# A diffusion trunk on one core: the gather of the experts placed right after the routing, the test for crowded groups placed ahead of the last scatter, and the last two experts' inner values transposed earlier

## The reference

```python
def _moe(h, router_w, router_b, w_gate, w_up, w_down):
    scores = jax.nn.sigmoid((t @ router_w).astype(jnp.float32))
    sel = scores + router_b.astype(jnp.float32)
    group_score = lax.top_k(sel.reshape(-1, N_GROUPS, EXPERTS_PER_GROUP), GROUP_SCORE_TOPK)[0].sum(-1)
    best_group = jnp.argmax(group_score, axis=-1)
    ...
    hid = jax.nn.silu(jnp.einsum("td,edf->tef", t, w_gate)) * jnp.einsum("td,edf->tef", t, w_up)
    out = jnp.einsum("tef,efd->td", hid * combine[..., None], w_down)
```

## Time and profile before

| | |
|---|---|
| median of three runs | 2187.74 us (2181.6 to 2188.81) |
| the profiled execution, its own time | 2186.74 us |
| its span in the trace | 2184.9 us |
| mean granted clock of TensorE | 0.973 |
| PE busy | 2021.1 us, 92% |
| DVE busy | 1338.0 us, 61% |
| ACT busy | 1034.3 us, 47% |

### The profile page before, as it was taken

How to read it: one execution, slowest core, us unless ns; L and a number is a source line. 1 busy time by engine, 2 the same in 40 slices (tenths; PEclk the granted TensorE clock), 3 DMA queues, 4 the chain that set the end, 5 groups by cost and what they waited for, 6 DMA issues and landing times.

```text
span 2184.9 us, 44966 instructions
## 1 busy us (share of the span) xinstructions
PE 2021.1 (92%) x18880; PEld 1403.4 (64%) x18881; DVE 1338.0 (61%) x2625; ACT 1034.3 (47%) x1783; POOL 246.5 (11%) x363
## 2 busy tenths in 40 slices
PE   6999999898998999899899998998999999988996
PEld 3666666557775675677666665776466666647774
DVE  2656665437896342689822325898656666537896
ACT  3334344226774341676523315766444444326774
POOL 1422222110001000100010001000322232110000
PEclk8999999998999999899999998999999999999998
DMA  9244344345886444488644353888311121125880
GB/s 392 90 152 153 123 146 156 141 156 187 282 322 216 159 172 158 162 309 300 240 150 146 138 190 123 310 303 283 121 46 63 47 70 46 45 80 186 282 303 29
DMA packets 56912, 381.22 MB, mean 174 GB/s; under 512 B 6400, under 2 KB 10624, under 8 KB 12144
## 3 DMA queue, kind: packets, MB, share of 16 engines
q1 hardware_dynamic: 51696, 373.00, 47.7%
q10 hardware_dynamic: 4608, 4.20, 0.6%
q0 software_dynamic: 384, 0.89, 0.1%
HBM read 373.96 MB, written 4.10 MB: 173 GB/s over the span
## 4 chain that ended last, share of the span: by engine, by line
PE 76%; DVE 13%; ACT 5%; issue 4%; DMA 2%; ACTq 0%; SPq 0%; DVEq 0%
PE ps L838 15%; PE ps L1505 6%; DVE e_wlo L2817 5%; PE ps L1509 5%; PE ps L1508 5%; PE ps L788 4%; PE ps L764 4%; PE ps L744 3%; PE ps L979 3%; PE ps L1292 3%; DVE bufx L2835 2%; PE ps L799 2%; PE ps L1461 2%; ACT e_whi L1685 2%; PE ps L1393 2%
## 5 line engine op out<-in xcount | busy, mean ns | idle before, releaser
L2817 DVE TENSOR_TENSOR e_wlo<-ring,e_whi 128x1024 fp32r<-128x1024 f32 x384 | 456.2, 1222 | 90.9 <-ACT e_whi L1685 75.2
L1685 ACT ACTIVATE e_whi<-ring 128x1024 fp32r<-128x1024 f32 x384 | 402.9, 1060 | 117.9 <-PE ps L1509 114.4
L838 PE MATMUL ps<-bufh,ring 128*128 128x384 f32 x1024 | 392.4, 505 | 2.0 <-ACT scratch L1685 0.7
L838 PEld LDWEIGHTS ps<-bufh,ring 128*128 128x128 f32 x1024 | 177.0, 191 | 93.9 <-issue 18.3
L1505 PE MATMUL ps<-e_whi,e_hs 128*128 128x512 f32 x512 | 210.5, 411 | 28.2 <-DVE e_wlo L2817 24.8
L1685 ACT ACTIVATE scratch<-ps 128x384 f32<-128x384 f32 (+6 forms) x311 | 109.0, 368 | 213.2 <-PE ps L838 53.3
L1509 PE MATMUL ps<-e_whi,e_hs 128*128 128x512 f32 x512 | 200.4, 391 | 0.0
L1508 PE MATMUL ps<-e_wlo,e_hs 128*128 128x512 f32 x512 | 200.0, 391 | 0.0
L2946 POOL TENSOR_SCALAR bufx<-bufo,x_gb 128x384 f32<-128x384 f32 x56 | 37.6, 685 | 1072.5 <-DVE bufo L2256 1072.5
L1505 PEld LDWEIGHTS ps<-e_whi,e_hs 128*128 128x128 f32 x512 | 96.0, 188 | 69.1 <-ACT e_whi L1685 43.1
L2349 DVE SCALAR_TENSOR_TENSOR scratch<-scratch,par 128x386 f32<-128x386 f32 x192 | 128.5, 669 | 4.8
(11 more groups left out here) (312 smaller groups left out, 3490.7 us busy)
## 6 DMA issues: line engine op xcount, KB each, us to landing
ring<-in_moe SPq DMA_DIRECT2D x192, 1024.0 KB, 4.9
ring<-in_w_ada SPq DMA_DIRECT2D x96, 1024.0 KB, 6.8
ring<-in_gdn_w_in SPq DMA_DIRECT2D x32, 1024.0 KB, 7.0
ring<-in_gdn_w_out SPq DMA_DIRECT2D x8, 1024.0 KB, 5.0
ring<-in_gqa_w_in SPq DMA_DIRECT2D x6, 1024.0 KB, 5.1
ring<-in_gqa_w_out SPq DMA_DIRECT2D x4, 1024.0 KB, 6.9
ring<-in_mla_w_out SPq DMA_DIRECT2D x4, 1024.0 KB, 7.7
ring<-in_mla_w_in SPq DMA_DIRECT2D x3, 1024.0 KB, 4.9
```

The costliest lines, as they stand in the source:

```text
L838: last = mm(ps[:, head_bank(n, m), 0:T], w[:, m % 2, kt, :], bufh[:, kt, :], start=(kt == 0), stop=(kt == KT - 1))
L1685: return op(out, in_, ACT.Copy, **kw)
L2817: return tt_(e_wlo[:, b, :], w, e_whi[:, b, :].bitcast(F32), ALU.subtract)
```

## The change

It has three parts, all in the mixture of experts.

1. The eight gather pieces of pair 0 leave the table and stand in the code of PE right behind the token tiles: four ahead of the counts and the row of slot numbers, four behind. ACT takes the first four, splits piece 0, copies the row ("r"), takes the other four, and goes on with piece 1.
2. The branch moves. On PE (`crowded_blocks`) and DVE it stands just ahead of the first scatter step of the last group, on ACT behind the last step of the table. The flags are computed later on DVE (`crowded_flags`), after the second pair's `e_pick`, and the two `put_back` go there too. The extra blocks use other buffers (`x_yhi`, `x_ylo`).
3. In the last stretch the transposes of experts 2 and 3 of group 3 move ahead: T(3, 2) behind U(3, 3), and T(3, 3) behind D(3, 1). Each T of an expert other than the group's first also waits for the low part of the transpose before it (`tlo`).

```diff
-MOE_STEPS = [("G", 0, m) for m in range(8)]
+MOE_STEPS = []
...
+    if _x == NE - 1:
+        MOE_STEPS.append(("T", NG - 1, EPG - 2))
     if _late:
         MOE_STEPS.append(("S", _group, 2 * _turn))
     if _x >= 2:
         MOE_STEPS.append(("D", (_x - 2) // EPG, (_x - 2) % EPG))
...
+    if _x == NE - 1:
+        MOE_STEPS.append(("T", NG - 1, EPG - 1))
     if _late:
         MOE_STEPS.append(("S", _group, 2 * _turn + 1))
-    if _x >= 1:
+    if 1 <= _x < NE - 1:
         MOE_STEPS.append(("T", (_x - 1) // EPG, (_x - 1) % EPG))
-MOE_STEPS += [("D", 3, 2), ("T", 3, 3), ("D", 3, 3)] + [("S", 3, q) for q in range(4)]
+MOE_STEPS += [("D", 3, 2), ("D", 3, 3)] + [("S", 3, q) for q in range(4)]
...
-MOE_FOLLOW, MOE_PIECE_OF = [], {}
+MOE_FOLLOW, MOE_PIECE_OF = [("g", 0, m, None) for m in range(4)], {}
...
+            if _p == 1:
+                MOE_FOLLOW.append(("r", 0, 0, None))
+                MOE_FOLLOW += [("g", 0, _m, None) for _m in range(4, 8)]
...
                 token_tile(5)
+                for m in range(4):
+                    gather_piece(l, 0, m)
 
                 pe.wait_ge(sid_ready, l + 1)
...
                 last.then_inc(row2_mm, 1)
+                for m in range(4, 8):
+                    gather_piece(l, 0, m)
...
                     elif kind == "T":
+                        if e:
+                            pe.wait_ge(F["tlo"], n)
                         transpose_hidden(F, n, e % 2)
...
                         if e == 0:
+                            if j == NG - 1:
+                                crowded_blocks(l, comb)
...
                         if j == 0:
                             pick_pair(1)
+                            dve.wait_ge(row2_ready, l + 1)
+                            dve.wait_ge(ax_ready, 2 * l + 2)
+                            put_back(0)
+                            put_back(1)
+                            crowded_flags(l)
...
                     elif kind == "s":
+                        if e == 0 and j == NG - 1:
+                            crowded_blocks(l)
```

More of the change, by code:

```diff
@@ L507, in trunk @@
         x_put = e_hs[:, 2, 1, 0:TT, :].rearrange("p a b -> p (a b)")
+        x_yhi, x_ylo = (e_hs[:, 1, half, :, :].rearrange("p k c -> p (k c)") for half in range(2))
         e_whi, e_wlo = sb("e_whi", [P, SPLITS, PIECE], F32R), sb("e_wlo", [P, SPLITS, PIECE], F32R)
@@ L1533, in scatter_piece @@
                     b = banks[ft % len(banks)]
-                    mm(ps[:, b, 0:T], e_yhi[:, P * ft:P * ft + P], put, start=True, stop=False)
-                    mm(ps[:, b, 0:T], e_ylo[:, P * ft:P * ft + P], put,
+                    hi, lo = (e_yhi, e_ylo) if S is F else (x_yhi, x_ylo)
+                    mm(ps[:, b, 0:T], hi[:, P * ft:P * ft + P], put, start=True, stop=False)
+                    mm(ps[:, b, 0:T], lo[:, P * ft:P * ft + P], put,
                        start=False, stop=True).then_inc(S["sc"], 1)
@@ L1597, in moe @@
                 last.then_inc(row2_mm, 1)
+                for m in range(4, 8):
+                    gather_piece(l, 0, m)
                 comb = e_rt[7].rearrange("p (t e) -> p t e", t=TT)
[L1599 to L1622, removed]
-                                pe.nop()
-                            with pe.Else():
-                                pe.sem_inc(X["ga"], 5)
-                                pe.sem_inc(X["tr"], EPG)
-                                pe.sem_inc(X["wfree"], EPG * PIECES)
-                                pe.sem_inc(X["sc"], KT)
@@ L2102, in y_high @@
                 for y in range(2):
-                    copy(e_yhi[:, 512 * y:512 * y + 512], ps[:, 3 + y, :]).then_inc(S["yhi"], 1)
+                    copy((e_yhi if S is F else x_yhi)[:, 512 * y:512 * y + 512], ps[:, 3 + y, :]).then_inc(S["yhi"], 1)
             def moe(l):
@@ L2735, in route @@
                 pick_pair(0)
-                dve.wait_ge(rk_mm, 2 * l + 2)
-                v.step(V.tensor_copy(e_cnt[:, :], ps[:, 2, 80:84]))
-                v.wait()
-                for b in range(2):
-                    ts_(flags[:, :, b], e_cnt[:, :], float(P * (b + 1)), None, ALU.is_gt)
-                v.step(V.tensor_reduce(m3[:, 46:47], e_cnt[:, :], AX.X, ALU.max))
-                v.wait()
-                ts_(flags[:, 0, 2:3], m3[:, 46:47], float(P), None, ALU.is_gt).then_inc(flags_ready, 1)
                 for n in range(2, 2 * TT):
@@ L2770, in route, with crowded_flags @@
                 dve.wait_ge(comb_ready, l + 1)
-                dve.wait_ge(row2_ready, l + 1)
+            def crowded_flags(l):
+                m3 = e_rt[9]
+                dve.wait_ge(rk_mm, 2 * l + 2)
+                v.step(V.tensor_copy(e_cnt[:, :], ps[:, 2, 80:84]))
+                v.wait()
+                for b in range(2):
+                    ts_(flags[:, :, b], e_cnt[:, :], float(P * (b + 1)), None, ALU.is_gt)
+                v.step(V.tensor_reduce(m3[:, 46:47], e_cnt[:, :], AX.X, ALU.max))
+                v.wait()
+                ts_(flags[:, 0, 2:3], m3[:, 46:47], float(P), None, ALU.is_gt).then_inc(flags_ready, 1)
             def pick_pair(pair):
```

94 lines of the change are left out of this document (64 added, 30 removed).

## The result

The changed kernel takes 2168.95 us, the median of 6 runs (2166.31 to 2177.65), and the kernel before, on the same chip, 2182.91 us (6 runs, 2180.86 to 2188.81). The ratio is 0.9925 with an interval of 0.9903 to 0.9947: by it the change saves 16.4 us, and anything from 11.6 to 21.2 fits the interval; the two medians differ by 14.0. The profiled execution took 2167.08 us with a span of 2165.3, where before it was 2186.7 and 2184.9. The direction is as predicted, and the time lies just inside the forecast's lower bound of 2168; the gain is twice the forecast 8.2 us.

A forecast was written before the change was run, and what follows sets the result against it. PE was taken to set the pace inside the mixture, with time to be had only at its two ends. 22.2 - 3.4 - 5.8 + 10 - 12.8 - 2 = 8.2 us gained, forecast 2180 us, range 2168 to 2190.

The forecast's parts named there:

- the head: Last token copy to first expert matmul: gathering at once takes 10.1 us a layer, gaining 22.2 us for four.
- the transposes: Last stretch: earlier transposes end PE's waits, about 1.0 us remains ahead of D(3, 3); gain 10 us for four.
- the clock at the tail: Behind D(3, 3): idle time brings half clock in the scatter; loss 2 us for four.
- Piece 1 and the moved work: Inside the mixture: later piece 1 loses 3.4 us, DVE's work moved to step "w" loses 5.8 us, for four.
- The branch at the tail: Ahead of the last scatter: DVE's branch makes the first addition 3.2 us later; loss 12.8 us for four.
- rival 4: Branch fetch at the tail waits behind weights: 2.05 us longer erases the gain, 4 us longer gives 2196; chance 0.10.
- rival 2: DVE's moved work is covered and the gather runs at full clock in all four layers; 2170 us; chance 0.10.
- Rival 1: At the tail the flag is loaded and the branch target fetched while D(3, 3) runs; 2167 us; chance 0.08.
- rival 3: Gather stays at half clock until the low half, or scatter and sums run at half clock; 2183 to 2187; chance 0.20.

The follow-up runs named there:

- e5: Changed kernel with the flags and two `e_put` on DVE moved from step "w" to between the splits of pieces 0 and 1; 2173.62 us, ratio 0.9922.
- e6: Changed kernel with ACT splitting piece 1 ahead of the row's copy and the four low gathered pieces; 2166.18 us, ratio 0.9921.
- e8: Changed kernel with DVE's moved work in the earlier gap, piece 1 split early and DVE's branch ahead of the last low output; 2158.64 us, ratio 0.9875.
- e1: Kernel before with only the last two transposes moved ahead; 2172.1 us, ratio 0.9948.
- e3: Changed kernel without flag loads, branches and the crowded-group blocks behind them, on all three engines; 2162.84 us, ratio 0.9898.
- e2: Changed kernel with the last two transposes back at their old place; 2187.02 us, ratio to before 1.0.
- e7: Changed kernel with DVE's branch one step earlier, ahead of the low part of the last group's output; 2172.98 us, ratio 0.9924.
- e9: Kernel of e8 with ACT's splits of pieces 0 and 1 still earlier, behind the third and sixth token tile's copies; 2157.65 us, ratio 0.9866.
- e4: Kernel before without flag loads, branches and crowded-group blocks, its gather still begun behind the counts; 2167.23 us, ratio 0.9921.

## Why the prediction was right in kind and half in size

The mechanisms were right; the step that failed is the sizing of three terms of the sum, each too pessimistic: the head's 10.1 us, the transposes' 10 us, and the 2 us for the clock at the tail.

*The head, 22.2 us: measured 25.0.* The mechanism was right (a branch of 3.4 to 3.8 us in the way, a gather that needs nothing behind it). Too large was the price of a head, 10.1 us each, with "half clock for most of the high half in two layers of the four": the changed kernel has 10.2, 10.0, 8.6 and 8.6. Two layers ran most of their high half at half clock, as I said. Full clock gives 8.6 and not 9.1: the counts and the row lie in 1.1 us between the two halves (501.51 to 502.61 in the first layer), where I took 1.6. That makes 2.0 us for four. Some 0.9 more is the half clock, which cost 1.6 and 1.5 us in its two layers where the mean of 10.1 stands for 2.0 each.

*Piece 1 and the moved work, 9.2 us: measured 8.6.* Right, and shown to be these two: e5 takes 4.7 of it back, e6 3.3, e8 8.35 with both.

*The transposes, 10 us: measured 13.0,* by e1 alone as well. The remaining wait was 0.81 to 0.88 us rather than 1.0, which is 0.7 of the 3.0. (The 1.0 was near, but the terms named for it, a low part, 1.39 and 1.22 us against PE's 2.8, do not add up to it.) The third layer of before had 1.4 us more to lose, its half-clock stretch behind the wait of 2.3 us: I priced the waits and not what they did to the clock behind them. The rest, some 0.2 a layer, is PE's busy time in the stretch, 10.59 us for 10.78 at the same number of matmuls.

*The branch at the tail, 12.8 us: measured 13.0,* and 12.8 by e3. Its parts were off in both directions. I had 5.5 us to the first addition in each layer, with DVE last; it was 6.2, 6.6, 5.6 and 4.4, with PE last in the first and fourth layers and DVE last in the second and third. The three tails in which the next layer's weights come in (DMA share 0.43 to 0.54) average 6.15 us and the last (0.05) has 4.4; e2, e5 and e6 show the same, 6.5 against 3.5, 6.0 against 4.8, 6.0 against 4.5. That fits rival 4's mechanism at under half its price, with the last layer shorter than my sum, so that the two cancelled: that the total came out at 13.0 was luck in part. The transfers of the instruction queues show it, on PE with 5.0 us where the fetch ended late and 3.4 where it did not, and on DVE in e7, where the transfer starts 2.4 to 2.7 us behind the branch in the first three layers and 1.2 in the last. But weights coming in do not always cost something: with DVE's branch out of the way, e7's second and third tails (4.8 us, DMA share 0.68) are no longer than its fourth (4.8, share 0.04), as PE is the last there, and PE's start was late only in the first (4.9 us for 3.6 to 3.7). Why the fetch of the first layer is the late one, in six of the seven kernels with the branch at the tail, stays open; no run took the weights away.

*The clock at the tail, 2 us: measured under 1, and already in the 13.0.* PE fell to half clock in three of four layers (0.69, 0.69, 0.75), as forecast. The scatter behind the first addition took 5.29 us at either clock, paced by DVE. Only the first matmuls ahead of that addition cost 0.4 us, in the two layers where PE came last. Behind the scatter little is lost either: the next matmul that reads streamed weights starts 7.60, 7.74 and 7.60 us behind the first addition, and 7.60 in all three before.

The errors, 2.8 + 0.6 + 3.0 + 2.0 - 0.2 = 8.2, are the whole gap from 8.2 to 16.4, as measured by stretches. No rival came true as a whole, and that the time is near rival 2's 2170 is chance. Rival 1 (the branch hides) is excluded by PE's idle 4.95 us, rival 2's covered work by e5, rival 3 by the clock of 0.79 to 1.00 in the head. About half of the gap, 4.3 us, has one root, the clock: I charged half clock too dear where PE comes out of idle time (0.9 at the head, 2.0 at the tail), and gave no credit for the clock where the change takes idle time away (1.4 in the third layer's last stretch). The other half is made of small sizes at full clock: 2.0 us at the head, 1.6 at the transposes, 0.6 in the middle.

The Trainium skill's 108 ns for a compare-and-branch ("Advanced Engine Details and Errata", section "Control Flow Timing") would have put the branch at 0.4 us for four layers, an estimate by that page; PE's rows have 3.4 to 5.0 us for each. By the page "Perfetto Trace Analysis" of the Trainium skill, section "Per-engine timelines", an instruction that still waits stands in a queue and the sequencer is ready for the next. The new place agrees with it no more than the old one did: PE's flag was loaded at 670.8, 1.7 us ahead of the end of D(3, 3), but only 0.16 us behind the split that its last waiting matmul needed. Matmuls that had nothing left to wait for did not hold the load.

## What to carry to other kernels

In this kernel a branch over rarely used code cost PE 3.3 to 5.0 us where it must go on, and DVE waits of up to 4.5. Put each engine's branch where that engine waits anyway, which need not be the same place (DVE's hid almost wholly in a wait of 2.7 us in e7; no such place was tried for PE). When a stall is removed, take off what it did to the clock behind it too, and when work is moved into a dense stretch look for a gap on that same engine first: here 1.45 us of DVE and two splits of ACT fitted into gaps at no cost, and, with DVE's branch, gained 8.9 us (e8) and 11.3 us (e9) by stretches on top of the change's 16.4. Judge edits of this size by stretches: the windows at full clock repeated within 0.2 us from run to run while whole executions moved by several.

## What the hardware showed unexpectedly

- The wait of 2.3 us ahead of D(3, 2) was followed by half clock in 1 of 4 layers of before, 4 of 4 in e2 and 3 of 4 in e4, each time for 1.3 us. What decides it stays open.
- The same unchanged routing code, first to last token copy, takes 5.4 us at full clock and up to 7.2 where much of it runs at half clock. Both ends occur in one execution, here e5's third and fourth layers:

```profile
1333.10:1340.40 7.30, 4.90 (x26) 4.26 (x24) 6.66 (x26) 3.39 (x7) 0.00 (x0) 0.67 0.00 0
1965.70:1971.10 5.40, 2.98 (x26) 2.50 (x23) 4.81 (x22) 3.11 (x7) 0.00 (x0) 1.00 0.00 0
```

- The cost of a branch is recorded in different places: on PE inside the compare-and-branch itself (3.4 to 5.0 us), on DVE as idle time behind it, put down to its sequencer (the 4.50 us above, while its compare-and-branch is recorded with 56 to 67 ns). Whoever adds up branch instructions misses DVE's and ACT's.
